# Moving one unit of gathered V rows from VectorE to TensorE in a PEER decoder layer

## The reference

```python
# h: (256, 2048); per token and head (8 heads) 16 experts of 16384 are picked
eid = i1 * N_KEYS + i2                      # N_KEYS = 128
g = softmax(best_s)
a  = gelu(einsum('td,thkd->thk', h, expert_u[eid]))     # a dot with a gathered row of expert_u
y  = einsum('thk,thkd->td', g * a, expert_v[eid])       # a weighted sum of gathered rows of expert_v
out = layernorm(ALPHA * h + y, ln2_g, ln2_b)
```

## Time and profile before

| | us |
|---|---|
| median of 3 runs | 1783.23 |
| profiled execution | 1784.41 |
| its span | 1782.6 |
| VectorE busy | 1400.2 |
| TensorE busy | 1462.4 |
| mean DMA rate over the span | 343 GB/s |

### The profile page before, as it was taken

One profiled execution on the slowest core, in us unless ns is written; L12 is line 12 of the kernel. 1 busy time (PEld: TensorE's weight loads), 2 busy tenths in 40 slices (PEclk: granted clock), 3 DMA queues, 4 the chain that ended last, 5 costly groups with the idle time before them and its releaser, 6 DMA issues.

```text
span 1782.6 us, 16637 instructions
## 1 busy us (share of the span) xinstructions
PE 1462.4 (82%) x6028; PEld 931.5 (52%) x6028; DVE 1400.2 (79%) x1940; ACT 384.3 (22%) x804; POOL 982.6 (55%) x591
## 2 busy tenths in 40 slices
PE   8999999999979708877767777788976899999900
PEld 7988999988668503333323333344536644444400
DVE  6666646676879998876788888677879797788998
ACT  5665464664101212102010102011111200000000
POOL 3210000000456677878776777888883187678881
PEclk9999999999989858989998899999995599999955
DMA  9876444474999999999999999999999399999994
GB/s 313 281 258 206 118 143 142 142 243 162 382 374 420 382 425 403 415 426 425 418 424 425 420 413 424 422 416 424 416 424 421 136 375 401 407 396 417 342 365 159
DMA packets 159810, 610.85 MB, mean 343 GB/s; under 512 B 21514, under 2 KB 74854, under 8 KB 97814
## 3 DMA queue, kind: packets, MB, share of 16 engines
q0 software_dynamic: 79232, 480.80, 66.5%
q1 hardware_dynamic: 80496, 128.99, 20.5%
HBM read 683.42 MB, written 2.10 MB: 385 GB/s over the span
## 4 chain that ended last, share of the span: by engine, by line
PE 26%; POOL 24%; DVE 18%; DMA 14%; issue 14%; DVEq 3%; ACT 1%; SPq 0%; POOLq 0%; ACTq 0%
PE psum_all L586 13%; POOL u_slot L524 13%; POOL v_slot L541 11%; DMA v_slot<-in_expert_v_dram,eid 10%; DVE xh L1778 6%; DVE u_slot L1743 6%; PE psum_all L726 4%; DMA u_slot<-in_expert_u_dram,eid 4%; DVEq L1770 1%; PE psum_all L751 1%; PE psum_all L707 1%; PE psum_all L611 1%; PE psum_all L613 1%; PE psum_all L937 1%; PE psum_all L962 1%
## 5 line engine op out<-in xcount | busy, mean ns | idle before, releaser
L1743 DVE SCALAR_TENSOR_TENSOR u_slot<-u_slot,xh 128x2048 f32<-128x2048 f32 x256 | 577.8, 2288 | 124.0 <-DMA u_slot<-in_expert_u_dram,eid 121.4
L962 PE MATMUL psum_all<-v_slot,diag 128*128 128x512 f32 x1024 | 509.2, 651 | 165.9 <-DMA v_slot<-in_expert_v_dram,eid 120.5
L524 POOL DMA_INDIRECT u_slot<-in_expert_u_dram,eid x256 | 446.2, 1743 | 282.1 <-DVE u_slot L1743 115.4
L541 POOL DMA_INDIRECT v_slot<-in_expert_v_dram,eid x240 | 466.2, 1942 | 150.8 <-DVEq L1779 81.9
L962 PEld LDWEIGHTS psum_all<-v_slot,diag 128*128 128x128 f32 x1024 | 204.1, 207 | 457.7 <-issue 235.6
L1778 DVE SCALAR_TENSOR_TENSOR xh<-v_slot,gate,xh 128x2048 f32<-128x2048 f32 x128 | 301.0, 2352 | 44.2 <-DMA v_slot<-in_expert_v_dram,eid 32.5
L1361 DVE TENSOR_TENSOR w_lo<-w_ring,w_hi 128x512 fp32r<-128x512 f32 x240 | 156.6, 688 | 77.6 <-ACT w_hi L1000 74.5
L586 PE MATMUL psum_all<-act_hi,w_hi 128*128 128x256 f32 x640 | 185.2, 289 | 1.3 <-DVE w_lo L1361 1.2
L586 PE MATMUL psum_all<-act_lo,w_hi 128*128 128x256 f32 x640 | 181.0, 283 | 0.0
L586 PE MATMUL psum_all<-act_hi,w_lo 128*128 128x256 f32 x640 | 180.4, 282 | 0.0
L1000 ACT ACTIVATE w_hi<-w_ring 128x512 fp32r<-128x512 f32 x240 | 139.4, 622 | 42.2 <-PE psum_all L586 42.0
(11 more groups left out here) (280 smaller groups left out, 1453.6 us busy)
## 6 DMA issues: line engine op xcount, KB each, us to landing
w_ring<-in_w_in_dram SPq DMA_DIRECT2D x88, 512.0 KB, 5.2
u_slot<-in_expert_v_dram SPq DMA_DIRECT2D x40, 1024.0 KB, 8.8
wo_ring<-in_w_out_dram SPq DMA_DIRECT2D x32, 512.0 KB, 5.5
wq_ring<-in_w_query_dram SPq DMA_DIRECT2D x32, 512.0 KB, 9.6
w_ring<-in_cmp_k_w_dram POOLq DMA_DIRECT2D x16, 512.0 KB, 5.9
w_ring<-in_cmp_v_w_dram POOLq DMA_DIRECT2D x16, 512.0 KB, 4.6
u_slot<-in_expert_u_dram,eid POOLq DMA_INDIRECT x256
v_slot<-in_expert_v_dram,eid POOLq DMA_INDIRECT x256
```

The lines of the kernel that those rows point to most:

```text
L524: nc.gpsimd.indirect_dma_start(out=u_slot[m % RU][:, :], out_offset=None, in_=expert_u[0], in_offset=bass.IndirectOffsetOnAxis(ap=eid[:, n ...
L541: nc.gpsimd.indirect_dma_start(out=v_slot[m % RV][:, :], out_offset=None, in_=expert_v[0], in_offset=src, bounds_check=ROWS - 1, oob_is_er ...
L962: ins = nc.tensor.matmul(bank[4 + q][:, :], diag[:, n % 2, k, :], v_slot[m % RV][:, 512 * q:512 * q + 512], start=(m == 0), stop=False)
L1743: V.scalar_tensor_tensor(u_slot[m % RU][:, :], u_slot[m % RU][:, :], 1.0, xh[:, n // PH, :], ALU.mult, ALU.mult, accum_out=u_dot[:, n, k:k ...
```

## The change

- TensorE takes units 0 to 8 of V and VectorE units 9 to 15 (`PE_PICKS` = 144 where it was 128). Unit 8 is accumulated in PSUM banks 0 to 3, where tile 1's dense sums then go on.
- After pick 127 TensorE adds ALPHA * h to tile 0's sums; ScalarE copies them to SBUF (`sum0`); tile 1's one-hot groups use banks 4 to 6 and `sum0` is later put back into banks 4 to 7 by four matmuls with the identity.
- V runs earlier against U: 4 // 3 where it was 11 // 8.
- Of tile 1's 16 one-hot groups 8 stand among the last dots (at picks 244 to 254) and 8 behind them; before it was 11 and 5. On TensorE 8 of them stand between the picks of unit 8 and 8 behind pick 143.
- The slabs have 6 slots (`RD`) where they had 8. The rows of gains and offsets of the second layer norm are loaded into two of the slots so freed, behind all slabs on the SyncE queue; before they were loaded as soon as TensorE had used V pick 127.
- The exponential of unit 15 and its gelu stand elsewhere on ScalarE, and VectorE takes the gates of unit 15 before V pick 160 and not right behind the last dot.
- Tile 0 is normalised by two operations over 2048 columns where it were eight over 512, tile 1's dense sums are added by one and not four, and tile 0 is written out by one transfer.

```diff
-HALF_U = TOPK * PH
+V0_PICKS = TOPK * PH
+PE_PICKS = V0_PICKS + TOPK
+RD = 6
-HOT1_AT = 15 * TOPK + 5
+HOT1_AT = {15 * TOPK + 4 + 3 * b // 2: b for b in range(NG_T // 2)}
...
-        sp.wait_ge(S["v_used"], HALF_U)
+        for f in range(FD):
+            if f < RD:
+                sp.wait_ge(S["dots_done"], TOPK * NU - RU + f + 1)
+            else:
+                sp.wait_ge(S["dense_used"], f - RD + 1)
+            first = ROWS + NKEY * f
+            sp.dma_start(u_slot[f % RD][:, :], expert_v[0][first:first + NKEY, :]).then_inc(s_d[f % RD], 16)
         for row, src in ((ln2g_sb, ln2_g), (ln2b_sb, ln2_b)):
             sp.dma_start(row[:, :], src.partition_broadcast(P).rearrange("p a d -> p (a d)")
                          ).then_inc(S["s_ln2row"], 16)
...
-            while sent < min(TOPK * NU, TOPK * AHEAD + (m + 1) * 11 // 8):
+            while sent < min(TOPK * NU, TOPK * AHEAD + (m + 1) * 4 // 3):
...
-        for m in range(HALF_U):
+        for m in range(PE_PICKS):
             n, k = divmod(m, TOPK)
             if k == 0:
                 pe.wait_ge(S["diag_ok"], n + 1)
             if m == 80:
                 pick_transposes(0)
-            if m >= 94 and m % 2 == 0 and m < 94 + 2 * NG_T:
-                dense_rows(0, (m - 94) // 2)
+            if m >= 97 and m % 2 and m < V0_PICKS:
+                dense_rows(0, (m - 97) // 2)
+            if m == V0_PICKS:
+                for q in range(4):
+                    ins = nc.tensor.matmul(bank[4 + q][:, :], ident_a[:, :], xh[:, 0, 512 * q:512 * q + 512],
+                                           start=False, stop=True)
+                ins.then_inc(S["t0_part"], 1)
+                pe.wait_ge(S["dense_ok"], NG_T)
+            if m == V0_PICKS + 4:
+                pe.wait_ge(S["part_ok"], 1)
+                pick_transposes(1)
+            if V0_PICKS + 5 <= m < V0_PICKS + 5 + NG_T // 2:
+                dense_rows(1, m - V0_PICKS - 5)
             pe.wait_ge(s_v[m % RV], 16 * (m // RV + 1))
...
+        for b in range(NG_T // 2, NG_T):
+            dense_rows(1, b)
+        pe.wait_ge(S["dense_ok"], 2 * NG_T)
         for q in range(4):
-            nc.tensor.matmul(bank[4 + q][:, :], ident_a[:, :], xh[:, 0, 512 * q:512 * q + 512], start=False, stop=False)
-        pick_transposes(1)
-        for b in range(NG_T):
-            dense_rows(1, b)
+            nc.tensor.matmul(bank[4 + q][:, :], ident[:, :], sum0[:, 512 * q:512 * q + 512], start=True, stop=False)
...
+            if b == 10:
+                diagonals(8)
             dense_out(0, b)
+        act.wait_ge(S["t0_part"], 1)
+        for q in range(4):
+            ins = nc.scalar.activation(sum0[:, 512 * q:512 * q + 512], bank[4 + q][:, :], ACT.Copy)
+        ins.then_inc(S["part_ok"], 1)
         unit(14)
+        expo_gate(15)
         picks_out(1)
         for b in range(NG_T):
-            if b == 11:
-                unit(15)
+            if b == NG_T // 2:
+                gelu_unit(15)
             dense_out(1, b)
...
-                if n and k == (10 if n < NU - 1 else 3):
+                if n and k == (10 if n < NU - 1 else 2):
                     gates_of(n - 1)
...
-        gates_of(NU - 1)
...
-        for m in range(HALF_U, TOPK * NU):
+        for m in range(PE_PICKS, TOPK * NU):
+            if m == PE_PICKS + TOPK:
+                gates_of(NU - 1)
...
-                norm_out(0, lambda q: bank[4 + q][:, :], y0)
+                root_inverse(0)
+                V.scalar_tensor_tensor(y0[:, :], psum_all[:, 4:8, :].rearrange("p a b -> p (a b)"), l2mv[:, 0, 0:1],
+                                       ln2g_sb[:, :], ALU.subtract, ALU.mult)
+                dve.drain()
+                V.scalar_tensor_tensor(y0[:, :], y0[:, :], l2rs[:, 0:1], ln2b_sb[:, :], ALU.mult, ALU.add
+                                       ).then_inc(S["final_ok"], 1)
```

More of the change, by code:

```diff
@@ L320, in build @@
     s_v = [nc.alloc_semaphore(f"s_v{i}") for i in range(RV)]
-    s_d = [nc.alloc_semaphore(f"s_d{i}") for i in range(RU)]
+    s_d = [nc.alloc_semaphore(f"s_d{i}") for i in range(RD)]
     def bview(i, *shape):
@@ L423, in _ @@
                          ).then_inc(S["s_ln2row"], 16)
[L424 to L437, removed]
+        sp.wait_ge(S["final_ok"], 1)
+        sp.dma_start(out_v[:, 0, :], y0[:, :]).then_inc(S["s_out"], 16)
+        for q in range(4):
+            sp.wait_ge(S["final_ok"], q + 2)
+            sp.dma_start(out_v[:, 1, 512 * q:512 * q + 512], xh[:, 1, 512 * q:512 * q + 512]).then_inc(S["s_out"], 16)
+        sp.wait_ge(S["s_out"], 16 * 5)
     @block.gpsimd
@@ L1791, in norm_out @@
             dve.drain()
-            for q in range(4):
-                cols = slice(512 * q, 512 * q + 512)
-                V.scalar_tensor_tensor(dst[:, cols], src(q), l2mv[:, t, 0:1], ln2g_sb[:, cols], ALU.subtract, ALU.mult)
-                dve.drain()
-                V.scalar_tensor_tensor(dst[:, cols], dst[:, cols], l2rs[:, t:t + 1], ln2b_sb[:, cols], ALU.mult, ALU.add
-                                       ).then_inc(S["final_ok"], 1)
-        def right_cols(q):
-            return xh[:, 1, 512 * q:512 * q + 512]
         V.memset(eps2[:, :], LN_EPS).then_inc(S["eps2_ok"], 1)
@@ L1826, in _ @@
                     hot_rows(0, HOT0_AT[m])
-                if m >= HOT1_AT:
-                    hot_rows(1, m - HOT1_AT)
-        gates_of(NU - 1)
-        for b in range(TOPK * NU - HOT1_AT, NG_T):
+                if m in HOT1_AT:
+                    hot_rows(1, HOT1_AT[m])
+        for b in range(NG_T // 2, NG_T):
             hot_rows(1, b)
@@ L1849, in _ @@
         for q in range(4):
-            V.bn_stats(l2st[:, 1, q, :], right_cols(q))
+            V.bn_stats(l2st[:, 1, q, :], xh[:, 1, 512 * q:512 * q + 512])
         stats_of(1)
-        norm_out(1, right_cols, xh[:, 1, :])
+        root_inverse(1)
+        for q in range(4):
+            cols = slice(512 * q, 512 * q + 512)
+            V.scalar_tensor_tensor(xh[:, 1, cols], xh[:, 1, cols], l2mv[:, 1, 0:1], ln2g_sb[:, cols], ALU.subtract, ALU.mult)
+            dve.drain()
+            V.scalar_tensor_tensor(xh[:, 1, cols], xh[:, 1, cols], l2rs[:, 1:2], ln2b_sb[:, cols], ALU.mult, ALU.add
+                                   ).then_inc(S["final_ok"], 1)
     block_cm.__exit__(None, None, None)
```

45 lines of the change are left out of this document (22 added, 23 removed).

## The result

The changed kernel took 1786.65 us (median of 20 runs, 1782.48 to 1788.85) where the kernel before took 1783.61 us (20 runs). The ratio is 1.0015, 95% interval 1.0009 to 1.0022: 0.15% slower, and not 1.25% faster. That is less than the 0.3% which the prediction took as the least that can be told; with 20 runs of each it is just clear of noise. The time lies outside the range of 1746 to 1783. The profiled execution took 1785.23 us with a span of 1783.5.

The account below looks back on a forecast made before the run. Transfers with one hole and an unfilled end were taken to bind. Of 39.5 us taken from VectorE, 18 are given back by the later start and 1.3 come from the norm: 1761 us, 22 us lower; range 1746 to 1783.

Parts of the forecast that it names:

- What bounds: From 500 us on, a stream of transfers with one hole and an unfilled end; only filling these gains.
- End of U: Sixteen V picks move before the last dot, which was put at 1394, 7 us later; bounds 1384 and 1414.
- byte account: Bytes landed by the last dot: V +5.9 MB, layer-norm rows -2.1, some 3.5 slabs -3.7; sum near zero, dot near 1392.
- TensorE in unit 8: Waits from pick 132, a few us at 1.2 GHz hidden by seven slots; V143 done at 1408, 14 after last dot.
- Groups behind pick 143: First group at full clock, others at 1.2 GHz; adds from 1431 (18 us later), slabs from 1441 (25 us later).
- Adds: Before pick 246: 37 at 2.47 us until 1523, 56 at 2.94, last 9 at 2.47; pick 246 at 1712.
- The 65 us: Adds keep their 2.47 us pace until slabs have pressed for about 65 us, from slab 6 at 1458 until 1523.
- Slabs, end, norm: Six slab slots cost nothing; tile 0's sums at 1703.5, before pick 246; wider norm operations save 1.3 us, end 47.5.
- Bytes only move: Rival: transfers bind throughout and the hole just comes later; last dot 1414, time 1781; chance 0.10.
- full clock in the packed groups: Rival: picks 140 to 143 leave the clock up; adds 6 us and slabs 11 us sooner, 1755; chance 0.17.
- late slab: Rival: with six slots slabs land in 15.2 us, tile 0's sums at 1728, end 1778; chance 0.06.
- unit 8 at 1.2 GHz throughout: Rival: low clock from pick 132's wait, V143 at 1456, U gathers held up, 1809, priced at 1800; chance 0.08.

Follow-up runs that it names:

- e1: Changed kernel, but its first six slabs are asked for only when the last dot is done; 1772.17 us, ratio 0.9945 to the kernel before.
- e6: Changed kernel, but only the first 1024 of 2048 columns of each slab are loaded; 1756.94 us, ratio 0.9849 to the kernel before.
- e5: Kernel before, with seven of its 128 adds put between last dot, unit 15's gates and last five one-hot groups; 1773.56 us, ratio 0.9943.
- e4: Kernel before, first eight slabs asked for only after the last dot, seven adds among the last one-hot groups; 1774.44 us, ratio 0.9947.
- e3: Changed kernel, first six slabs asked for only after the last dot, adds 144 to 150 among last one-hot groups; 1762.55 us, ratio 0.9883.

## Why the prediction was wrong

The span came out 24.0 us above the forecast: 12.1 for the last dot, 0.7 from it to the first add, 11.1 for the adds to pick 246, and 0.1 for the end. Two steps failed.

**What bounds.** Right as far as it was said: a stream of transfers with a hole and an unfilled end. The forecast did not keep to it, as the steps below show.

**End of U: the step that failed first.** The last dot was put at 1394; it came at 1406.1, 19.5 us later than before, where 7 were forecast and 27.7 was the bound. The byte account let only "some 3.5 slabs" land before it. All six were asked for before it (the last at 1396.0) and landed within 8.2 to 10.1 us, and V144 and V145 were sent before it as well (1387.7 and 1392.9). By my own account these are 2.5 slabs and, from V143 on, three V picks more, 4.8 MB or an estimated 11 us at 424 GB/s: nearly all of the 12. The rows for this were at hand: the earlier trace rows had slabs landing in 8.7 us beside full queues of gathers. I used them to say that slabs are never late, and not to ask whom they pass. With the slabs held back (e1) the last dot came at 1394.3, the forecast instant. That is luck: there dots and one-hot groups set it, with the DMA share at 0.66 and 0.69, and not the bytes of the account.

**TensorE in unit 8.** Near: a wait at pick 132 (10.8 us), low clock for some picks, V143 done 16.3 us behind the last dot where 14 were forecast. It did not hold up U by itself (e1).

**Groups behind pick 143.** Right in mechanism and size: 3.45 us for a packed group at 1.2 GHz; adds 37.7 us behind the last dot (37 forecast), first slab 47.8 us behind it (47). TensorE ran one-hot groups for 20.7 us in a row, and the granted clock stayed 0.50. By the Trainium skill ("TensorE: Matmul & The Clock Gate", Part 1) sustained matmuls open the gate; the trace does not agree for these. The clock rose while the four matmuls of `sum0` ran (6.07 us), and the slabs' matmuls behind them ran at the full clock from the start.

**Adds: the second step that failed.** I let 37 adds run at 2.47 us, then 56 at 2.94, and the last nine at 2.47 again. Measured: 102 in 292.1 us, 2.86 each, against 2.75 forecast, 11 us more; in e1 it was 292.7 us. It was 19 at full pace (to 1491.3), then 75 at 3.00 us each, then 8 at full pace:

```profile
1480.00:1500.00 20.00, 15.91 (x8) 1.00 1.00 412
...
1716.11 19.68 DVE L1795 SCALAR_TENSOR_TENSOR xh<-v_slot,gate,xh 128x2048 f32<-128x2048 f32 x8 [0.50 <-DMA v_slot<-in_expert_v_dram,eid]
```

So the term that was too large is the full pace behind the first late slab. The 65 us were a misreading: I took the edge of a window in the earlier trace rows, 1500, for the instant at which the adds slow down. The 24 adds of the earlier trace rows end at 1472.3, and the next one already waited for its rows, 37 us behind slab 8 (asked for at 1435.6). VectorE was busy for 17.8 and 15.7 us of 20 in these two windows of the kernel before, in the columns of the earlier trace rows:

```profile
1460.00:1480.00 20.00, 20.00 (x48) 8.78 (x47) 17.76 (x8) 0.00 (x0) 17.56 (x9) 1.00 1.00 392
1480.00:1500.00 20.00, 20.00 (x48) 8.93 (x47) 15.66 (x8) 0.00 (x0) 17.86 (x8) 1.00 0.98 393
```

In the changed kernel full pace lasted 20 us behind slab 6 (asked for at 1471.2). Why 20 and not 37 is not shown. That it is the transfers that slow the adds is shown: the DMA share is full from 1480 to 1736, and in e6, with 21 MB less to move, the same adds took 255 us. The whole picks of unit 15 were sent from 1700.7 on, right behind the last slab and the layer-norm rows (1698.2), while VectorE was waiting for rows; before, more than 50 us lay between the last slab (sent at 1648.4) and them. So of the 39.5 us taken from VectorE nothing was left: VectorE no longer was what the tail waited for.

**Slabs, end, norm.** Right: the slabs' matmuls ran without a gap (234 instructions in the window from 1500 to 1600, as before), pick 246 did not wait for TensorE, the end was 47.6 us (47.5 forecast), the two wide operations took 2.35 us each.

**Rivals.** "Bytes only move" gave 1414 for the last dot and 1781 for the time. Its picture is the one that held: the hole came later, the transfers bound behind it, nothing was gained. It had 0.10. Its parts were off, though: the last dot came 8 us sooner than it said, and the time was still 6 us above it, as the hole also grew. The other three did not happen: no full clock in the packed groups, no late slab, no unit 8 at 1.2 GHz throughout.

What stays open: what TensorE's waits for one-hot groups in unit 8 and its spells at 1.2 GHz cost by themselves was not tried, and parts of the change as the 4 // 3 order of V and U were not undone alone.

## What to carry to other kernels

When work is moved off a busy engine, ask first what the transfers do: if the same bytes cross the same hole, the engine's time comes back as waiting, and the gain lies in what keeps the queues filled there. Here seven adds put into idle time gave 10.7 us with no unit moved (e5); beside such adds and late slabs the moved unit was worth 11.9 us more (e4 to e3). A load that is asked for early because its slot is free can overtake one that is needed now; ask for it when the urgent ones have landed. And read a short landing time under full traffic twice: that load is there soon, and others wait longer for it. An instant at which something slows down is read from single instructions, not from the edge of a window.

## What the runs showed of the hardware

1 MB loads from SyncE's queue landed in 8.2 to 10.1 us in full traffic, while the last U gather, sent before four of them from GpSimd's queue, took 31.5 us (sent at 1372.3, landed at 1403.8); with the six held back the last two U gathers took 16.2 and 15.7 us. Holding them back brought the last dot 11.8 us forward; their 6.3 MB are 15 us at 424 GB/s. Matmuls of 40 columns kept TensorE busy for 20.7 us in a row without the clock rising from 1.2 GHz, and the same matmuls took 1.9 us a group when picks of 512 columns stood between them.
